# 96 instead of 88 tokens by gathered expert rows, and dense expert products over 160 instead of 168 columns

## The chip, the cores and the metric

The kernel runs on one core of one Trainium2 chip. The metric is the device time of one execution in microseconds, the median of several runs. Everything below is read from one profiled execution, with times in microseconds (us) from the start of its span.

## What is computed

The reference is three transformer layers over 256 tokens of width 1024, in float32. The first has two kinds of attention, the second a state-space mixer, both with a squared-ReLU feed-forward layer. The third has a short convolution and window attention, and then the layer this change is about: a product of experts (PEER) with 16384 experts, of which each token takes 16 in each of 8 heads, 128 in all.

```python
def peer_ffn(h, wq, keys, u_tab, v_tab):        # u_tab, v_tab: 16384 x 1024
    ...
        q = (ht @ wq).reshape(t, PEER_HEADS, 2, PEER_DK)
        sa = jnp.einsum('thd,hnd->thn', q[:, :, 0], keys[0])
        sb = jnp.einsum('thd,hnd->thn', q[:, :, 1], keys[1])
        va, ia = lax.top_k(sa, PEER_TOPK)
        vb, ib = lax.top_k(sb, PEER_TOPK)
        ...
        top, pos = lax.top_k(cand, PEER_TOPK)
        eidx = jnp.take_along_axis(cidx, pos, axis=-1)
        g = jax.nn.softmax(top, axis=-1)
        u = u_tab[eidx]
        v = v_tab[eidx]
        a = jax.nn.gelu(jnp.einsum('thkd,td->thk', u, ht))
        return jnp.einsum('thk,thkd->td', g * a, v)
```

## The kernel before

The kernel is one program with an instruction list written out for each engine; the engines meet by counted semaphores, and each works its list strictly in order. There is no scheduler. The first 750 us are the first two layers and the attention of the third; the change touches none of it. The expert layer divides the 256 tokens in two.

**Dense tokens.** For the first ND tokens (168) all 16384 experts are computed. The table u comes in 128 units of 512 KB (`peer_u`), v in 128 units (`peer_v`). The hidden activations X have a place for 128 x ND numbers on each partition, and what isn't chosen is multiplied by a gate of zero. `u_unit` makes 8 float32 matmuls of 128 x ND for one unit; each shows as two records in the trace. The gates are made by "spreads": for 4 tokens at a time, `one_hot` builds one-hot rows from the chosen numbers (VectorE, GpSimd and ScalarE share this), 4 matmuls of 128 x 128 make the gate matrix of these tokens in PSUM, and VectorE (`empty_gates`, `u_late`) and ScalarE multiply it onto X. There are ND / 4 spreads.

**Gathered tokens.** For the other tokens (88) only the chosen expert rows are read. One "pass" handles 128 chosen rows, so there are as many passes for u as tokens, and again as many for v. GpSimd issues an indirect DMA of 128 rows of 4 KB (`gather`) into one of four slots; VectorE then multiplies the slot with the token's row and sums it (u, `scalar_tensor_tensor` over 1024 elements at L2206) or adds the slot, scaled, to an accumulator (v, L1429). A gather may be issued when the pass four before it is done:

```python
if n >= 4:
    e.wait_ge(*rows_v["pass", n - 4])
```

The passes are in four groups by `ROW_FIRST = (0, 32, 64, 80, 80 + LAST_ROWS)`: in the last one, LAST_ROWS tokens (8) have their 128 choices divided into LAST_PARTS (16) parts over the partitions.

**The order of the work** comes from the constants `N_FIRST` (16), `N_BETWEEN` (23), `N_LATE` (100) and `N_EARLY` (42), by hand-written loops:

- Choice of experts: VectorE finds the top 16 (`pick`), with passes 0 to 15 between; TensorE meanwhile does the first 42 units of u.
- Gate stage: passes 16 to 22, then `spread_steps`. That is a list of 4 x 43 = 172 half units of u, over which the spreads and the passes 23 to N_LATE - 1 are laid:

```python
if (row - N_BETWEEN) * (n_left - 12) < (i - 3) * (N_LATE - N_BETWEEN) and row < N_LATE:
    yield "row", row
```

  The dense products of two units take a PSUM bank (two banks take turns); the bank is free when ScalarE's gelu has been made, and that waits for VectorE where the X of the same place is to be gated.
- Down stage (`down_T`): 256 chunks of v, each half a unit. ScalarE rounds a chunk to its high part (`w_hi`), VectorE makes the low part (`w_lo`, L1423), and TensorE makes for each of 4 blocks a product of w_hi with high and low part of X (2 x ND columns) and one of w_lo with the high part (ND columns). Four chunks can be cut ahead. In VectorE's list the passes from N_LATE on stand between the chunks:

```python
def pass_step(n):
    return 1 + 250 * (n - N_LATE) // (N_PASS - N_LATE)
```

SyncE loads the units in order, each when its raw buffer is free: four buffers for u, eight for v.

Of the kernel before, what the change touches and what calls it, by code (L numbers as in the profile page):

```python
# [21 lines left out]
NHL = 4  # L22
AHEAD = 3
N_EARLY = 42
ND = 168
LAST_ROWS = 8
LAST_PARTS = 128 // LAST_ROWS

OFF_X = 0
# [110 lines left out]
def build(nc, T, out):  # L140
    with ExitStack() as ctx:
        build_in(ctx, nc, T, out)


def build_in(ctx, nc, T, out):
# [82 lines left out]
    def sm(name, p1=128):  # L228
        o, n = SML[name]
        return ar[0:p1, OFF_SM + o:OFF_SM + o + n]  # L230
# [48 lines left out]
    first_v = next(i for i, x in enumerate(plan) if x[0] == "peer_v")  # L279
    DEEP = (128 * ND, OFF_GB + 1024, OFF_HN, OFF_HN + 1024)  # L280

# [249 lines left out]

    X = V(0, 128, ND)
    hT5 = V(20480, 8, 256)
    QP, SCO = 28672, 24576
    hU = V(SCO, 8, ND)

    row_h = [V(SCO + 2048, 1024), V(SCO + 3072, 1024), V(22528, 1024), V(23552, 1024)]
    row_acc, row_out = row_h, V(0, 8, 256)

    ROW_FIRST = (0, 32, 64, 80, 80 + LAST_ROWS)  # L540
    ROW_SUMS = {(24, 0): (0, LAST_ROWS + 16), (48, 0): (1, LAST_ROWS + 48), (60, 0): (2, LAST_ROWS)}
    N_ROWS = ROW_FIRST[4]
    row_g, row_a = [stat(f"rows {n}", N_ROWS) for n in ("gates", "products")]
    row_at = V(OFF_SM + SML["lre"][0], 96)[:, 0:N_ROWS]
    part_rows, part_own, part_sum = sm("cmask"), sm("bones")[:, 0:8], sm("bones")[:, 8:24]
    last_own, last_sum = sm("bones")[:, 24:24 + LAST_PARTS], sm("bones")[:, 24 + LAST_PARTS:24 + LAST_PARTS + LAST_ROWS]
    part_h, last_h, last_rows = V(12288, 8, 128), V(8192, 8, 128), V(9728, 128)

    passes = [("u", p) for p in range(N_ROWS)] + [("v", p) for p in range(N_ROWS)]
    nth = {x: n for n, x in enumerate(passes)}  # L550
    N_PASS, N_FIRST, N_BETWEEN, N_LATE, N_ONES = len(passes), 16, 23, 100, 3
    U_COPY = N_EARLY + 4

    def row_group(p):
# [47 lines left out]
    def spread_steps():  # L602

        n_left, s, emptied, known, late, due, queue = 4 * (64 - N_EARLY // 2), 0, 0, N_EARLY // 2, None, [], []
        n_spread = ND // 4
        i, row = 0, N_BETWEEN
# [33 lines left out]
        assert row == N_LATE and emptied == n_spread  # L640
        yield "late", late, ND

    def sync_program(e):
        e.dma_start(V(OFF_SM, SM_FIRST), T["small"][:, 0:SM_FIRST]).then_inc(small_in, 16)
        e.wait_ge(x_in[0], 16)
        for i, (_, source, _, _) in enumerate(plan):
# [3 lines left out]
            if i == first_v:  # L650
                for s in range(ND // 4 - len(ONES_AT), ND // 4):
                    e.wait_ge(*mm_done["spread", s])
# [766 lines left out]
    def vector_program(e):  # L1419
# [735 lines left out]
        def row_indices():  # L2155
# [8 lines left out]
            own, three = V(OFF_HN + 512, 3, 8, 16), V(OFF_HN + 896, 3, 16)  # L2164
            own2, three2 = V(9216, 3, LAST_PARTS, LAST_ROWS), V(9600, 3, LAST_ROWS)
            e.wait_ge(*mm_done["parts"])
# [1300 lines left out]
```

## Time and profile before

| | |
|---|---|
| median of 3 runs | 1417.73 us (1416.06 to 1417.78) |
| the profiled execution's own time | 1416.42 us |
| its span, first to last instruction | 1414.4 us |
| mean granted TensorE clock | 0.997 of full speed |
| busy: TensorE matmul, VectorE, ScalarE, GpSimd | 1378.1, 1138.3, 775.9, 465.1 us |
| transfers | 371.78 MB, mean 263 GB/s |
| software queue (the gathers) | 97.02 MB |

An engine's busy time is the union of its instructions' records. A matmul's record is longer than the distance to the next one, so the distance of starts tells the pace. What ended an idle time is written in brackets behind a row as the releaser.

### The profile page before, as it was taken

Reading aid. Unit: us, or ns where it says so; the run is one execution under the profiler, and the core shown is the slowest. Engines: PE = TensorE matmul, PEld = TensorE weight load, DVE = VectorE, ACT = ScalarE, POOL = GpSimd, SP = SyncE. Lnnn points to the kernel's source line nnn. Section 1 sums busy time; section 2 is a strip of 40 time slices with the busy share of each in tenths; the row PEclk is TensorE's granted clock in tenths of the full one; section 3 lists DMA queues with packets and bytes.
Section 4 is the critical chain, followed back from the end, with each engine's and each line's share of the span. In section 5 each row is a group of like instructions: output and inputs, shape, how many; then the busy total and the mean of one; then the engine's idle time right before and its main releaser. Section 6 shows DMA issues by size and latency. Waiting matters only on the chain.

```text
span 1414.4 us, 28160 instructions
## 1 busy us (share of the span) xinstructions
PE 1378.1 (97%) x10837; PEld 1283.3 (91%) x10837; DVE 1138.3 (80%) x2315; ACT 775.9 (55%) x1576; POOL 465.1 (33%) x436
## 2 busy tenths in 40 slices
PE   9899999998999999999999999899999999999998
PEld 7678998877889998888889999899999999999998
DVE  5776996787768889877667999576777699999997
ACT  6875886853255455577464301234333366666665
POOL 7700001000200000001100033688878358567671
PEclk9999999999999999999999999999999999999999
DMA  8305554652369899853444599999999999999994
GB/s 269 97 16 183 175 173 146 193 183 64 126 209 348 311 332 333 311 160 108 123 134 137 166 353 368 364 353 384 381 376 369 376 391 402 399 369 394 398 379 158
DMA packets 102579, 371.78 MB, mean 263 GB/s; under 512 B 11424, under 2 KB 11568, under 8 KB 102320
## 3 DMA queue, kind: packets, MB, share of 16 engines
q1 hardware_dynamic: 68096, 245.71, 49.2%
q0 software_dynamic: 26576, 97.02, 18.0%
q10 hardware_dynamic: 7776, 27.27, 5.4%
q8 instruction: 88, 1.44, 0.4%
q14 instruction: 43, 0.35, 0.1%
HBM read 368.90 MB, written 1.05 MB: 262 GB/s over the span
## 4 chain that ended last, share of the span: by engine, by line
PE 80%; DVE 12%; ACT 3%; DMA 2%; issue 2%; POOL 1%; DVEq 0%; SPq 0%; ACTq 0%
PE ps L668 78%; DVE arena L1423 4%; DVE w_lo L1423 2%; DVE arena L2206 1%; DMA arena<-in_u_rows,arena 1%; ACT arena L2350 1%; ACT w_hi L2353 1%; PE ps L886 1%; DVE arena L2109 1%; DVE arena L2033 1%; DVE arena L2031 1%; DVE arena L2030 1%; DMA arena<-in_peer_v 1%; ACT arena L2353 1%; PE ps L1013 0%
## 5 line engine op out<-in xcount | busy, mean ns | idle before, releaser
L2353 ACT ACTIVATE w_hi<-arena 128x512 fp32r<-128x512 f32 x680 | 422.4, 627 | 270.4 <-PE ps L668 254.5
L1423 DVE TENSOR_TENSOR w_lo<-arena,w_hi 128x512 fp32r<-128x512 f32 x680 | 454.7, 691 | 136.2 <-ACT w_hi L2353 132.9
L668 PE MATMUL ps<-act_hi_lo,w_hi 128*128 128x256 f32 (+1 forms) x2496 | 546.3, 313 | 4.8 <-DVE w_lo L1423 2.2
L668 PE MATMUL ps<-arena 128*128 128x168 f32 (+7 forms) x4798 | 469.9, 279 | 17.2 <-ACT arena L2350 7.4
L668 PEld LDWEIGHTS ps<-arena 128*128 128x128 f32 (+3 forms) x4798 | 442.8, 166 | 39.3 <-issue 21.1
L668 PE MATMUL ps<-act_hi_lo,w_lo 128*128 128x168 f32 (+1 forms) x1760 | 455.1, 259 | 0.1
L668 PEld LDWEIGHTS ps<-act_hi_lo,w_hi 128*128 128x128 f32 x2496 | 421.1, 190 | 10.1 <-issue 4.2
L668 PEld LDWEIGHTS ps<-act_hi_lo,w_lo 128*128 128x128 f32 x1760 | 336.7, 191 | 0.2 <-issue 0.2
L668 PE MATMUL ps<-w_hi,act_hi_lo 128*128 128x512 f32 (+2 forms) x960 | 300.7, 389 | 7.5 <-DVE w_lo L1423 3.2
L3270 POOL DMA_INDIRECT arena<-in_v_rows,arena x88 | 190.4, 2163 | 111.5 <-DVE arena L1429 105.5
L668 PEld LDWEIGHTS ps<-w_hi,act_hi_lo 128*128 128x128 f32 x960 | 179.3, 188 | 49.0 <-issue 9.7
L1423 DVE TENSOR_TENSOR arena<-arena 128x512 f32<-128x512 f32 (+16 forms) x306 | 182.0, 603 | 43.8 <-ACT arena L2350 36.8
L668 PE MATMUL ps<-w_lo,act_hi_lo 128*128 128x512 f32 (+2 forms) x480 | 184.7, 385 | 0.0
L3270 POOL DMA_INDIRECT arena<-in_u_rows,arena x88 | 104.3, 1185 | 172.9 <-DVE arena L2029 92.8
L2353 ACT ACTIVATE arena<-ps 128x512 f32<-128x512 f32 (+20 forms) x160 | 70.9, 459 | 135.7 <-DVE arena L1423 102.4
L2350 ACT ACTIVATE arena<-arena 128x128 f32<-128x128 f32 (+9 forms) x247 | 119.4, 498 | 43.8 <-DVE arena L1423 21.3
L2206 DVE SCALAR_TENSOR_TENSOR arena<-arena 128x1024 f32<-128x1024 f32 x88 | 108.8, 1240 | 36.5 <-DMA arena<-in_u_rows,arena 33.5
L2350 ACT ACTIVATE arena<-ps 128x512 f32<-128x512 f32 (+24 forms) x141 | 54.6, 417 | 150.4 <-PE ps L668 126.0
L1429 DVE SCALAR_TENSOR_TENSOR arena<-arena 128x1024 f32<-128x1024 f32 (+5 forms) x110 | 117.0, 1064 | 3.7 <-DMA arena<-in_v_rows,arena 2.9
L668 PEld LDWEIGHTS ps<-w_lo,act_hi_lo 128*128 128x128 f32 x480 | 90.3, 188 | 16.6
L3281 POOL TENSOR_SCALAR arena<-arena 128x128 f32<-128x128 f32 x63 | 83.4, 1328 | 3.1 <-DVE arena L2124 1.5
L3099 POOL TENSOR_TENSOR act_hi_lo<-arena,act_hi_lo 128x256 fp32r<-128x256 f32 x4 | 4.1, 1022 | 242.6 <-ACT act_hi_lo L2353 242.6
(106 smaller groups left out, 723.6 us busy)
## 6 DMA issues: line engine op xcount, KB each, us to landing
arena<-in_w_ff SPq DMA_DIRECT2D x128, 512.0 KB
arena<-in_peer_u SPq DMA_DIRECT2D x128, 512.0 KB
arena<-in_peer_v SPq DMA_DIRECT2D x128, 512.0 KB
arena<-in_w_ada ACTq DMA_DIRECT2D x48, 512.0 KB, 6.5
arena<-in_w_glu SPq DMA_DIRECT2D x16, 512.0 KB
arena<-in_peer_wq SPq DMA_DIRECT2D x16, 512.0 KB
arena<-in_w_in SPq DMA_DIRECT2D x12, 512.0 KB
arena<-in_w_conv SPq DMA_DIRECT2D x12, 512.0 KB
```

Source lines behind the costliest of these rows:

```text
L668: return e.matmul(o, l, r, start=start, stop=stop)
L886: ins = e.transpose(pb(bk, 2 * nk, 128)[:, h * nk + kb, :], att.s(u)[:, h, kb * 128:(kb + 1) * 128], ident)
L1423: return e.tensor_tensor(o, a, b, op)
L1429: return e.scalar_tensor_tensor(out=o, in0=a, scalar=s, in1=b, op0=op0, op1=op1)
L2030: lambda src, tv, ti, tmp: e.max_index(ti[:, 0:8].bitcast(U32), tv[:, 0:8], src),
L2031: lambda src, tv, ti, tmp: e.match_replace(tmp, tv[:, 0:8], src, NEG * 10),
L2033: lambda src, tv, ti, tmp: e.max_index(ti[:, 8:16].bitcast(U32), tv[:, 8:16], tmp)]
L2206: ins = e.scalar_tensor_tensor(out=slot, in0=slot, scalar=1.0, in1=row_h[g], op0=ALU.mult, op1=ALU.mult, accum_out=a)
L2350: return e.activation(o, a, f, **k)
L2353: return e.activation(o, a, ACT.Copy)
L3270: e.indirect_dma_start(row_slot(n), None, T[f"{kind}_rows"], bass.IndirectOffsetOnAxis(ap=row_at[:, p:p + 1].bitcast(U32), axis=0)).then_i ...
L3281: ins = e.tensor_scalar(ob[:, k, :], iota, ibT[:, n:n + 1], gT[:, n:n + 1], ALU.is_equal, ALU.mult)
```

## The change

Eight tokens go from the dense part to the gathered one: ND is 160, LAST_ROWS 16, LAST_PARTS therefore 8. There are 96 passes for u and 96 for v (88 before), 40 spreads (42 before), and N_LATE is 108, so that 85 passes lie in the spread steps (77 before) and 84 in the down stage (76 before). X is 8 columns narrower.

```diff
@@ -22,8 +22,8 @@
 NHL = 4
 AHEAD = 3
 N_EARLY = 42
-ND = 168
-LAST_ROWS = 8
+ND = 160
+LAST_ROWS = 16
 LAST_PARTS = 128 // LAST_ROWS
@@ -548,7 +548,7 @@
     passes = [("u", p) for p in range(N_ROWS)] + [("v", p) for p in range(N_ROWS)]
     nth = {x: n for n, x in enumerate(passes)}
-    N_PASS, N_FIRST, N_BETWEEN, N_LATE, N_ONES = len(passes), 16, 23, 100, 3
+    N_PASS, N_FIRST, N_BETWEEN, N_LATE, N_ONES = len(passes), 16, 23, 108, 3
     U_COPY = N_EARLY + 4
```

VectorE's list at the start of the spread steps, before and after in one piece. L2206 is a pass of u; a TENSOR_TENSOR of 128x512 with the TENSOR_SCALAR behind it is a one-hot; one that reads ps is the gating of a spread, and the 128x2x4 and 128x2x8 are `u_late`, which ScalarE's next gelu waits for.

```order
 L1423 TENSOR_TENSOR arena<-ps,arena 128x48x4
+L2206 SCALAR_TENSOR_TENSOR arena<-arena 128x1024
 L1423 TENSOR_TENSOR arena<-arena 128x2x4
-L2206 SCALAR_TENSOR_TENSOR arena<-arena 128x1024 x2
+L2206 SCALAR_TENSOR_TENSOR arena<-arena 128x1024
 L1423 TENSOR_TENSOR arena<-arena 128x512
 L1426 TENSOR_SCALAR arena<-arena 128x128
 L1423 TENSOR_TENSOR arena<-ps,arena 128x50x4
+L2206 SCALAR_TENSOR_TENSOR arena<-arena 128x1024
 L1423 TENSOR_TENSOR arena<-arena 128x2x8
-L2206 SCALAR_TENSOR_TENSOR arena<-arena 128x1024
```

A pass now stands ahead of `u_late` at these places, and there are more passes for each one-hot.

GpSimd's list at the same place: the gathers (L3270) and the one-hots (L3281). First before, then after.

```order
L3270 DMA arena<-in_u_rows,arena 128x1024 x7
L3281 TENSOR_SCALAR arena<-arena 128x128 x2
L3270 DMA arena<-in_u_rows,arena 128x1024 x2
L3281 TENSOR_SCALAR arena<-arena 128x128
L3270 DMA arena<-in_u_rows,arena 128x1024
L3281 TENSOR_SCALAR arena<-arena 128x128 x2
```

```order
L3270 DMA arena<-in_u_rows,arena 128x1024 x7
L3281 TENSOR_SCALAR arena<-arena 128x128 x2
L3270 DMA arena<-in_u_rows,arena 128x1024 x2
L3281 TENSOR_SCALAR arena<-arena 128x128
L3270 DMA arena<-in_u_rows,arena 128x1024 x3
L3281 TENSOR_SCALAR arena<-arena 128x128 x2
```

Here three gathers stand between two one-hots where there was one; up to this place the lists are the same.

VectorE's list in the middle of the down stage, first before, then after. L1429 is a pass of v, w_lo the low part of a chunk.

```order
L1429 SCALAR_TENSOR_TENSOR arena<-arena 128x1024
L1423 TENSOR_TENSOR w_lo<-arena,w_hi 128x512 x3
L1423 TENSOR_TENSOR act_hi_lo<-arena,act_hi_lo 128x2x168
L1423 TENSOR_TENSOR w_lo<-arena,w_hi 128x512
L1429 SCALAR_TENSOR_TENSOR arena<-arena 128x1024
L1423 TENSOR_TENSOR w_lo<-arena,w_hi 128x512 x3
L1423 TENSOR_TENSOR act_hi_lo<-arena,act_hi_lo 128x2x168
```

```order
L1429 SCALAR_TENSOR_TENSOR arena<-arena 128x1024
L1423 TENSOR_TENSOR w_lo<-arena,w_hi 128x512 x3
L1423 TENSOR_TENSOR act_hi_lo<-arena,act_hi_lo 128x2x160
L1429 SCALAR_TENSOR_TENSOR arena<-arena 128x1024
L1423 TENSOR_TENSOR w_lo<-arena,w_hi 128x512 x3
L1429 SCALAR_TENSOR_TENSOR arena<-arena 128x1024
```

Before, a pass came every three or four chunks; after, nearly always every three.

## Rows read from the trace of the kernel before

**Rows 1.** The page, the span in 40 equal slices.

```profile
PE   9899999998999999999999999899999999999998
...
DVE  5776996787768889877667999576777699999997
...
GB/s 269 97 16 183 175 173 146 193 183 64 126 209 348 311 332 333 311 160 108 123 134 137 166 353 368 364 353 384 381 376 369 376 391 402 399 369 394 398 379 158
```

**Rows 2.** Windows: busy us (instructions) of each engine, granted clock, DMA share, GB/s.

```profile
core 0: us, PE busy (x) PEld busy (x) DVE busy (x) ACT busy (x) POOL busy (x), PEclk, DMA share, GB/s
877.00:1126.00 249.00, 242.91 (x1755) 241.45 (x1755) 172.17 (x328) 87.51 (x260) 186.10 (x147) 0.99 0.98 370
940.00:1100.00 160.00, 160.00 (x1179) 160.00 (x1178) 119.44 (x231) 60.82 (x184) 132.05 (x106) 1.00 1.00 378
900.00:910.00 10.00, 9.54 (x70) 9.24 (x68) 4.73 (x7) 0.00 (x0) 3.46 (x4) 1.00 1.03 409
1127.00:1403.00 276.00, 275.73 (x2072) 275.43 (x2073) 270.76 (x397) 183.49 (x317) 170.78 (x72) 1.00 0.96 373
```

**Rows 3.** Groups by form, TensorE, 940 to 1100 us: busy, mean ns, idle before.

```profile
L668 PE MATMUL ps<-arena 128*128 128x168 f32 x931 | 138.0, 306 | 0.0
L668 PE MATMUL ps<-arena 128*128 128x128 f32 x248 | 32.7, 275 | 0.0
```

**Rows 4.** Timeline of TensorE: start, duration, and idle time before it.

```profile
877.19 0.55 PE L1203 MATMUL ps<-arena 128*128 128x128 f32 x3 [1.35 <-DVE arena L1423]
...
914.97 20.30 PE L668 MATMUL ps<-arena 128*128 128x168 f32 x134 [5.43 <-ACT arena L2350]
...
1200.41 0.35 PE L668 MATMUL ps<-act_hi_lo,w_hi 128*128 128x336 f32 x1
...
1200.60 0.24 PE L668 MATMUL ps<-act_hi_lo,w_lo 128*128 128x168 f32 x1
...
1200.68 0.35 PE L668 MATMUL ps<-act_hi_lo,w_hi 128*128 128x336 f32 x1
```

**Rows 5.** Timeline of VectorE: passes 22, 28, 36, 55 and 99.

```profile
895.63 1.22 DVE L2206 SCALAR_TENSOR_TENSOR arena<-arena 128x1024 f32<-128x1024 f32 x1 [0.95 <-DMA arena<-in_u_rows,arena]
...
911.53 1.23 DVE L2206 SCALAR_TENSOR_TENSOR arena<-arena 128x1024 f32<-128x1024 f32 x1 [1.32 <-DMA arena<-in_u_rows,arena]
...
935.37 1.23 DVE L2206 SCALAR_TENSOR_TENSOR arena<-arena 128x1024 f32<-128x1024 f32 x1 [1.07 <-DMA arena<-in_u_rows,arena]
...
986.49 1.22 DVE L2206 SCALAR_TENSOR_TENSOR arena<-arena 128x1024 f32<-128x1024 f32 x1
...
1111.28 1.27 DVE L1429 SCALAR_TENSOR_TENSOR arena<-arena 128x1024 f32<-128x1024 f32 x1
```

**Rows 6.** GpSimd: one gather's row, and groups by form, 940 to 1100 us.

```profile
902.25 0.94 POOL L3270 DMA_INDIRECT arena<-in_u_rows,arena  x1 [1.61 <-DVE arena L2206]
...
L3281 POOL TENSOR_SCALAR arena<-arena 128x128 f32<-128x128 f32 x48 | 62.4, 1306 | 1.2
L3270 POOL DMA_INDIRECT arena<-in_u_rows,arena x47 | 59.5, 1266 | 20.2 <-DVE arena L2206 12.6 <-issue 7.6
L3270 POOL DMA_INDIRECT arena<-in_v_rows,arena x11 | 13.0, 1186 | 6.6 <-DVE arena L1429 4.6 <-issue 1.3 <-DVE arena L2206 0.5
```

**Rows 7.** Groups by form, VectorE, 940 to 1100 us: the passes of u.

```profile
L2206 DVE SCALAR_TENSOR_TENSOR arena<-arena 128x1024 f32<-128x1024 f32 x50 | 62.3, 1248 | 15.1 <-DMA arena<-in_u_rows,arena 12.2 <-issue 2.6
```

**Rows 8.** Timeline of TensorE: the last dense u products, ending at 1125.84.

```profile
1109.70 16.14 PE L668 MATMUL ps<-arena 128*128 128x168 f32 x112
```

**Rows 9.** Down stage, VectorE: groups of 1140 to 1380, two rows of its timeline.

```profile
L1423 DVE TENSOR_TENSOR w_lo<-arena,w_hi 128x512 fp32r<-128x512 f32 x221 | 142.9, 689 | 3.0 <-ACT w_hi L2353 2.5 <-issue 0.3
...
L1423 DVE TENSOR_TENSOR act_hi_lo<-arena,act_hi_lo 128x336 fp32r<-128x336 f32 x55 | 27.8, 506 | 0.0
...
1385.90 1.28 DVE L1429 SCALAR_TENSOR_TENSOR arena<-arena 128x1024 f32<-128x1024 f32 x1
1387.09 1.29 DVE L1423 TENSOR_TENSOR w_lo<-arena,w_hi 128x512 fp32r<-128x512 f32 x2
```

## The prediction

> **What bounds the kernel now.** I read the page's slices first. From slice 23 on (815 us) TensorE, VectorE and the transfers are all near their tops at once [rows 1], so the share of busy time doesn't say who sets the pace, and the stages have to be read apart. All of the change lies in three of them: the choice of experts (778 to 877 us), the gate stage (877 to 1126 us: dense products with peer_u, one-hot "spreads", row passes 16 to 99) and the down stage (1127 to 1403 us: dense products with peer_v, row passes 100 to 175).
>
> The windows of the last two come next [rows 2]. In the gate stage TensorE is busy 243 of 249 us, VectorE 172, GpSimd 186. In the down stage TensorE is busy all the time, and VectorE 270.8 of 276 us. So TensorE sets the pace in both, but in the down stage VectorE has only 5.2 us to spare in 276, and in the gate stage two things stand close behind TensorE: the ring of four gather slots, and GpSimd.
>
> The ring is seen in the passes' own rows [rows 5]. A pass can start when its gather has landed; the gather into the same slot, four passes on, is issued when the pass is done. Pass 22 starts at 895.63 and pass 28 at 911.53: six periods of 2.65 us, and in this stretch every pass waits for its gather (each row ends with a DMA releaser). The loop is closed by the gather issued at 902.25, which releases pass 28 9.3 us later [rows 5, 6]. TensorE stops for 5.4 us before 914.97 [rows 4], because the gating on VectorE stands behind those passes in its queue. Passes 36 to 55 (935.37 to 986.49, 19 periods) still come every 2.69 us, behind their due time. Over the whole stage, passes 22 to 99 take 77 periods of 2.80 us. In 940 to 1100 VectorE stands 12.2 us before passes for gathers [rows 7].
>
> **What the change takes from TensorE.** In the gate stage the dense product has 8 columns fewer. 931 records of 168 columns and 248 of 128 fill 160 us [rows 2, 3]; taken in proportion to columns a record of 168 is 0.143 us, one of 128 0.109 us, and one of 160 0.136 us. The 86 units of this stage have 16 records each: 1376 x 0.0067 = 9.2 us less. Spreads go from 42 to 40, 8 records of 0.109 us each: 1.7 us less. Together 10.9 us. The first 42 units save another 4.5 us, but they run beside the choice of experts, where VectorE is the chain (TensorE waits for it 1.35 us at 877 [rows 4]), so I count them at nothing; if they were on the path, they would be worth 4.5 us at most.
>
> In the down stage one pair of products (336 and 168 columns) starts every 0.27 us at the full clock [rows 2, 4], where 504 columns at 2.4 GHz make 0.21. What the rest is the trace doesn't say. If it stays, 24 columns fewer save 0.010 us a pair, and 1024 pairs 10.2 us; if the second product is bound by its weight load, only 16 columns count, 6.8 us. The Trainium skill (TensorE: Matmul & The Clock Gate, Back-to-back issue gap) gives N/2.4 + 2.5 ns for one product, so by an estimate from that page the pair would take 0.215 us; the trace has 0.27, and the saving by the page's rule is again 0.010 us a pair.
>
> **What it adds.** 8 passes on expert rows of u and 8 of v, each with a gather of 512 KB. N_LATE goes from 100 to 108, so that 85 instead of 77 passes stand in the spread steps and 84 instead of 76 in the down stage.
>
> *Gate stage.* The steps are 172 half units, and the passes are laid over the first 160 of them. A half unit is 8 records of 0.143 and its share of the spreads, 0.21: 1.36 us now, 1.29 then. So passes are due every 2.83 us now and every 2.43 then. The ring must be asked whether it can do 2.43. It has never done so over a stretch: 2.65 at the start, 2.69 in passes 36 to 55. GpSimd has in 940 to 1100 per pass a gather (72.5 us over 58) and its share of the one-hots (62.4 us over 58), 2.33 us, and 0.15 us of issue ahead of each gather (8.9 us over 58) [rows 6]; with fewer one-hots for each pass (40 spreads for 85 passes, 42 for 77) that is 1.25 + 0.93 + 0.15 = 2.33 us, 96% of the due rate. The transfers would have to bring 262 KB of weights in each half unit and 278 KB of rows, 0.54 MB in 1.29 us: 418 GB/s, where the best ten microseconds here have 409 and the stage 370 [rows 2]. Nothing here can do the due rate with ease, so I take the ring's measured 2.65 us. Pass 22 stays where it is (the order up to it is unchanged), so pass 107 comes at 895.6 + 85 x 2.65 = 1120.9. Eleven half units of the program stand behind the last u-stage pass (now 14.6 us from 1111.28 to TensorE's last product at 1125.84 [rows 5, 8]; 11 x 1.36 = 15). TensorE can be up to two PSUM banks ahead of a late VectorE; I take 5 half units of lead, 6 x 1.29 = 7.7 us remain. End 1128.6 against 1125.8: **+2.8 us**. With no lead it is +9, with 8 half units -1. The bounds of the ring: 2.43 (it keeps the due rate: -10.9) and the stage's own mean of 2.80 (+15.5).
>
> *Down stage.* VectorE does 8 passes more. Two start-to-start distances behind a pass are 1.19 us (1385.90 to 1387.09 [rows 9]), so +9.5 us. The low part of the gates (act_hi_lo) has 320 elements instead of 336; 512 take 689 ns and 336 take 506 [rows 9], so 16 elements are 17 ns, over 64 of them -1.1 us. Against 5.2 us to spare that leaves +3.2 us, and as some idle time at the stage's ends can't be used I take **+4 us**. TensorE's 7 to 10 us are then of no use, it waits for w_lo. Bounds: +2, if all of VectorE's idle time fills and its tail is shorter; +8.4, if none fills. Transfers need per chunk of 1.11 us 262 KB and a third of 524 KB, about 395 GB/s, less than the 409 that were carried, and the ring has four periods of 3.3 us there for a gather that took 9.3, so I put nothing there.
>
> *The rest.* The reduction of the last group has 48 outputs instead of 24, three small operations are wider: at most 0.1 us in the chain at 812. Output: the last products have 16 columns instead of 8, the copies out 160 and 96 instead of 168 and 88: nothing.
>
> **Sum**: 2.8 + 4 = +6.8 us. The profiled execution took 1416.42 us, which gives 1423.2; the median of the runs is 1.3 us above it, 1424.5. I forecast 1424.
>
> **Rivals.** (1) *The gathers keep up.* When TensorE and its weights slow down for a moment, the ring gets more of the transfers and heals itself. Then the gate stage gains its 10.9 us, the down stage loses 4: -7, 1411 us. For it: passes 22 to 99 came every 2.80 us on average where 2.83 were due, so the late start was made up. Against it: the 418 GB/s. The Trainium skill (DMA: Bandwidth & Descriptors, Where 436 GB/s comes from) has two figures: about 358 GB/s from HBM, which ten microseconds of 409 contradict, and a fabric ceiling of 435. By the ceiling 418 would fit, and this rival would hold. Chance 0.2. (2) *The ring runs at 2.56 us*, the shortest distance that repeats while gathers are waited for: 895.6 + 217.6 + 7.7 = 1120.9, -4.9, and with the down stage -1: 1417. Chance 0.15. (3) *The ring stretches* to 2.80: more one-hots, gathers and weights collide, +15.5 + 4: 1437. For it: the gather took 9.3 us where the transfers were at 409 GB/s. Chance 0.15. (4) *VectorE is no floor in the down stage*, because its records are longer than what it really needs: then TensorE's 7 to 10 us come through, with +2.8 before them -4 to -7: 1411 to 1413. Against it: the start-to-start distances count, not the durations, and they fill the stage. Chance 0.05. My forecast keeps 0.45.
>
> **How the numbers follow.** The measurement tells 0.2% (2.8 us) from no change. Faster: rivals 1 and 4, 0.24 with a little of 2. Same, 1415 to 1420.5: rival 2 and the low edge of the forecast, 0.2. Slower: most of the forecast and rival 3, 0.56. The forecast's own range is 1418 to 1431. To leave out no more than 2 in 10 the range has to take in rival 1 at 1411 and reach to rival 3: 1410 to 1436.
>
> **What would show it.** The dense record of 160 columns at 0.136 us in its spacing, and a pair of the down stage at 0.257 to 0.26 us where nothing waits. Pass 22 still near 895, passes then every 2.65 us and nearly all of them waiting for a gather, TensorE with stops of several us in the gate stage (5.4 now). The last dense u product at about 1128. In the down stage VectorE at 99% or more and TensorE with small stops for w_lo, 280 us long. The prediction is wrong if passes come every 2.45 us without waits (rival 1), or if the down stage is shorter than 276 us (rival 4).

## The result: slower by 16 us, and the profile after

| | before | after |
|---|---|---|
| median | 1417.76 us (4 runs, 1416.06 to 1421.73) | 1433.89 us (4 runs, 1433.29 to 1440.20) |
| ratio to before | 1 | 1.0121, 95% interval 1.0103 to 1.0138 |
| span of the profiled execution | 1414.4 us | 1431.5 us |
| mean granted TensorE clock | 0.997 | 0.993 |

The change is slower, as forecast, and the time is inside the range. But the loss is 16.1 us where the forecast of 1424 had 6.3. The span grew by 17.1 us.

The page's slices of the changed kernel (40 slices of the span, busy share in tenths; the last line is what the transfers moved):

```profile
PE   9899999998999999999999998899999899999998
...
DVE  5766996788669889867668898567777699999998
...
GB/s 267 96 21 182 176 176 148 192 179 45 152 222 348 312 325 342 261 164 103 120 157 154 182 384 329 361 400 377 368 382 386 368 387 398 400 391 397 402 390 180
```

TensorE, at 9 in nearly all slices before [rows 1], now has gaps in the gate stage, and the transfers run at 387 to 402 GB/s in the slices of the down stage, the last one left out (369 to 402 before). The windows of the same kernel, with the columns of [rows 2]: the gate stage, its middle, its busiest ten microseconds, the down stage.

```profile
877.00:1136.00 259.00, 238.56 (x1739) 235.63 (x1739) 178.33 (x341) 80.56 (x250) 190.74 (x153) 0.97 0.97 370
940.00:1100.00 160.00, 151.42 (x1133) 150.29 (x1132) 115.22 (x230) 51.70 (x168) 128.69 (x102) 0.99 0.99 380
900.00:910.00 10.00, 9.97 (x76) 9.70 (x75) 4.94 (x8) 1.33 (x3) 3.52 (x4) 1.00 1.02 412
1138.30:1414.00 275.70, 273.28 (x2030) 266.08 (x2031) 272.56 (x396) 178.53 (x310) 198.43 (x80) 0.99 1.00 389
```

In the gate stage TensorE stands for 20.4 of 259 us, where it stood for 6.1 of 249. In the down stage the roles have changed: VectorE has 3.1 us of gaps (5.2 before), TensorE 2.4 (0.3 before).

VectorE's timeline of the changed kernel gives the passes. These are pass 22, the next two, pass 28 (911.09), and the last four of the gate stage up to pass 107:

```profile
898.24 1.23 DVE L2206 SCALAR_TENSOR_TENSOR arena<-arena 128x1024 f32<-128x1024 f32 x1 [3.50 <-DMA arena<-in_u_rows,arena]
...
900.67 1.23 DVE L2206 SCALAR_TENSOR_TENSOR arena<-arena 128x1024 f32<-128x1024 f32 x1 [1.20 <-DMA arena<-in_u_rows,arena]
...
903.18 1.23 DVE L2206 SCALAR_TENSOR_TENSOR arena<-arena 128x1024 f32<-128x1024 f32 x1 [1.27 <-DMA arena<-in_u_rows,arena]
...
911.09 1.23 DVE L2206 SCALAR_TENSOR_TENSOR arena<-arena 128x1024 f32<-128x1024 f32 x1 [1.31 <-DMA arena<-in_u_rows,arena]
...
1118.10 2.67 DVE L1429 SCALAR_TENSOR_TENSOR arena<-arena 128x1024 f32<-128x1024 f32 x2
...
1123.23 1.28 DVE L1429 SCALAR_TENSOR_TENSOR arena<-arena 128x1024 f32<-128x1024 f32 x1
...
1125.00 1.28 DVE L1429 SCALAR_TENSOR_TENSOR arena<-arena 128x1024 f32<-128x1024 f32 x1
```

From pass 22 to pass 107 are 85 periods in 226.8 us, 2.67 each. The group of the same passes in 940 to 1100 shows who made them late (12.2 us of waiting for gathers before [rows 7]):

```profile
L2206 DVE SCALAR_TENSOR_TENSOR arena<-arena 128x1024 f32<-128x1024 f32 x58 | 72.1, 1250 | 32.0 <-DMA arena<-in_u_rows,arena 31.8
```

The chain that ended last, between 870 and 1136 us of the changed kernel, shows the loop of the ring: a gather is issued by GpSimd (L3270), lands some 8 to 9 us later, a pass runs, and the next gather is issued, with one-hots (L3281) between (columns: start, duration, what). TensorE is in it at the very end only, for 3.3 us.

```profile
889.87 1.63 POOL arena L3270
891.80 8.85 DMA arena<-in_u_rows,arena
900.67 1.25 DVE arena L2206 x2
902.18 8.89 DMA arena<-in_u_rows,arena
911.09 1.25 DVE arena L2206 x2
913.58 2.88 POOL arena L3281 x2
916.62 1.83 POOL arena L3270
```

TensorE's timeline at both ends of the gate stage (changed kernel): the first stop for the gating, as long as before (5.24 against 5.43 us [rows 4]), the last stops, and the start of the down stage. The stop before 1123.32 ends when GpSimd's one-hots are done (1121.63 to 1123.22), which stand in its list behind a gather's issue.

```profile
899.79 12.43 PE L668 MATMUL ps<-arena 128*128 128x160 f32 x92
917.45 17.84 PE L668 MATMUL ps<-arena 128*128 128x160 f32 x111 [5.24 <-ACT arena L2350]
...
1117.83 3.31 PE L668 MATMUL ps<-arena 128*128 128x160 f32 x24 [0.57 <-ACT arena L2350]
1123.32 12.38 PE L668 MATMUL ps<-arena 128*128 128x128 f32 x88 [2.18 <-issue]
1138.25 0.44 PE L668 MATMUL ps<-act_hi_lo,w_hi 128*128 128x320 f32 x1 [2.55 <-DVE act_hi_lo L1423]
1138.48 0.34 PE L668 MATMUL ps<-act_hi_lo,w_lo 128*128 128x160 f32 x1
1138.62 0.55 PE L668 MATMUL ps<-act_hi_lo,w_hi 128*128 128x320 f32 x1
...
1139.10 0.55 PE L668 MATMUL ps<-act_hi_lo,w_hi 128*128 128x320 f32 x1
```

The last dense u product ends at 1135.70 (before at 1125.84 [rows 8]). The down stage's first product comes 2.55 us later (before 1.32), and its pairs start 0.48 us apart for the first 3.3 us, with TensorE's granted clock at half after the stops; at 1141.5 they go back to 0.26. VectorE waits there for a high part from ScalarE, which waits for TensorE:

```profile
1141.02 0.69 DVE L1423 TENSOR_TENSOR w_lo<-arena,w_hi 128x512 fp32r<-128x512 f32 x1 [1.02 <-ACT w_hi L2353]
```

What the down stage's first product waits for is the first load of peer_v, then its cutting (2.6 us in both kernels). SyncE issues it in its order behind the last load of peer_u, and that one waits until TensorE has freed a buffer, at 1126.64 in the changed kernel and 1116.22 before. The same piece of the chain in the changed kernel, then in the kernel before:

```profile
1127.11 8.50 DMA arena<-in_peer_v
```

```profile
1116.70 7.80 DMA arena<-in_peer_v
```

TensorE's own last four units take 9.1 us from there, 9.6 before, so it has to stop in both kernels, and its narrower products only make the stop longer.

From its first product to the first transpose of the output the down stage takes 286.8 us, 280.9 before. So the 17.1 us of the span are 9.9 in the gate stage, 1.2 at the change of stages and 6.0 in the down stage.

VectorE's groups in the down stage, 1150 to 1390 us, of the changed kernel. No wait is left but 1.1 us:

```profile
L1423 DVE TENSOR_TENSOR w_lo<-arena,w_hi 128x512 fp32r<-128x512 f32 x217 | 139.9, 684 | 1.1 <-ACT w_hi L2353 1.1
L1429 DVE SCALAR_TENSOR_TENSOR arena<-arena 128x1024 f32<-128x1024 f32 x70 | 89.5, 1278 | 0.0
L1423 DVE TENSOR_TENSOR act_hi_lo<-arena,act_hi_lo 128x320 fp32r<-128x320 f32 x55 | 26.6, 484 | 0.0
```

### The profile page after: what moved, and what is told of

Same layout as the page of the kernel before. It is cut to its first block, busy times and chain, and to the rows that moved or that the text cites. A ratio compares the mean times of both kernels' runs of the same rounds, so it can differ in the third digit from the quotient of the medians.

```text
span 1431.5 us, 28153 instructions
## 1 busy us (share of the span) xinstructions
PE 1375.1 (96%) x10821; PEld 1270.6 (89%) x10821; DVE 1151.5 (80%) x2333; ACT 767.1 (54%) x1568; POOL 496.3 (35%) x449
## 4 chain that ended last, share of the span: by engine, by line
PE 65%; DVE 15%; DMA 9%; POOL 5%; issue 4%; ACT 3%; DVEq 0%; SPq 0%; ACTq 0%
PE ps L668 63%; DMA arena<-in_u_rows,arena 6%; DVE arena L1423 5%; POOL arena L3270 3%; DVE arena L2206 2%; POOL arena L3281 2%; DVE w_lo L1423 2%; ACT arena L2350 1%; DMA arena<-in_v_rows,arena 1%; ACT w_hi L2353 1%; DVE arena L1429 1%; PE ps L886 1%; DVE arena L2109 1%; ACT arena L2353 1%; DMA arena<-in_peer_v 1%
## 5 line engine op out<-in xcount | busy, mean ns | idle before, releaser
L668 PE MATMUL ps<-arena 128*128 128x160 f32 (+8 forms) x4782 | 464.1, 279 | 29.8 <-ACT arena L2350 17.0
L668 PEld LDWEIGHTS ps<-arena 128*128 128x128 f32 (+3 forms) x4782 | 434.3, 168 | 54.7 <-issue 34.2
L668 PE MATMUL ps<-act_hi_lo,w_lo 128*128 128x160 f32 (+1 forms) x1760 | 451.8, 257 | 0.5 <-DVE w_lo L1423 0.5
L3270 POOL DMA_INDIRECT arena<-in_v_rows,arena x96 | 220.7, 2299 | 86.8 <-DVE arena L1429 79.9
L3270 POOL DMA_INDIRECT arena<-in_u_rows,arena x96 | 116.9, 1218 | 184.6 <-DVE arena L2029 92.7
L2353 ACT ACTIVATE arena<-ps 128x512 f32<-128x512 f32 (+19 forms) x158 | 70.2, 460 | 184.0 <-DVE arena L1423 153.0
L2206 DVE SCALAR_TENSOR_TENSOR arena<-arena 128x1024 f32<-128x1024 f32 x96 | 118.5, 1242 | 52.8 <-DMA arena<-in_u_rows,arena 52.6
L1429 DVE SCALAR_TENSOR_TENSOR arena<-arena 128x1024 f32<-128x1024 f32 (+6 forms) x118 | 127.0, 1076 | 3.2 <-DMA arena<-in_v_rows,arena 2.6
L2350 ACT ACTIVATE arena<-ps 128x512 f32<-128x512 f32 (+25 forms) x141 | 53.7, 412 | 122.3 <-PE ps L668 121.8
L3099 POOL TENSOR_TENSOR arena<-arena 128x32 f32<-128x32 f32 (+1 forms) x130 | 55.6, 442 | 81.4 <-ACT arena L2353 46.4
```

What stands on the lines that cost most here:

```text
L668: return e.matmul(o, l, r, start=start, stop=stop)
L1429: return e.scalar_tensor_tensor(out=o, in0=a, scalar=s, in1=b, op0=op0, op1=op1)
L2206: ins = e.scalar_tensor_tensor(out=slot, in0=slot, scalar=1.0, in1=row_h[g], op0=ALU.mult, op1=ALU.mult, accum_out=a)
L2350: return e.activation(o, a, f, **k)
L2353: return e.activation(o, a, ACT.Copy)
L3099: return e.tensor_tensor(o, a, b, op)
```

## The experiments

"u end" is the end of the last dense u product; "down stage" is from its first product to the first transpose of the output; a period is from pass 22 to the last pass of the gate stage, over their number. "First search" is the start of VectorE's first search for the largest scores (MAX8, L2029 before and after), which stands before anything that the change or an experiment touches. All in us, from the profiled execution; times are medians beside runs of the kernel before on the same chip. Two kernels had one run only, and no interval.

| run | time | ratio (95%) | first search | pass 22 | period | u end | down stage |
|---|---|---|---|---|---|---|---|
| before | 1417.8 to 1419.2 | 1 | 743.4 | 895.6 | 2.80 | 1125.8 | 280.9 |
| after | 1433.9 | 1.0121 (1.0103 to 1.0138) | 744.3 | 898.2 | 2.67 | 1135.7 | 286.8 |
| late100 | 1425.3 | 1.0046 (1.0028 to 1.0064) | 744.1 | 898.5 | 2.76 | 1120.6 | 295.0 |
| wide_columns | 1434.6 | 1.0100 (1.0064 to 1.0136) | 744.0 | 896.7 | 2.72 | 1140.2 | 286.1 |
| half_gathers | 1412.2, one run |  | 744.0 | 896.3 | 2.46 | 1115.9 | 285.6 |
| five_slots | 1421.8 | 1.0026 (1.0009 to 1.0042) | 747.1 | 899.1 | 2.51 | 1123.4 | 286.8 |
| pool_relief | 1426.8 | 1.0059 (1.0038 to 1.0080) | 744.6 | 897.3 | 2.59 | 1127.9 | 285.6 |
| five_relief | 1418.8 | 0.9997 (0.9979 to 1.0015) | 743.8 | 897.9 | 2.50 | 1120.1 | 286.6 |
| half_v_passes | 1422.3, one run |  | 743.3 | 897.6 | 2.67 | 1135.9 | 275.6 |
| five_slots_168 | 1421.4 | 1.0023 (0.9999 to 1.0048) | 745.5 | 898.5 | 2.79 | 1128.3 | 282.0 |
| narrow_only | 1418.0 | 0.9991 (0.9962 to 1.0021) | 746.4 | 898.8 | 2.76 | 1122.3 | 295.6 |
| narrow_gate | 1416.4 | 0.9983 (0.9961 to 1.0005) | 744.3 | 898.4 | 2.74 | 1122.1 | 284.2 |
| narrow_down | 1426.8 | 1.0034 (1.0008 to 1.0061) | 742.6 | 894.6 | 2.77 | 1122.5 | 295.4 |
| narrow_half_v | 1406.3 | 0.9913 (0.9887 to 0.9940) | 744.4 | 898.1 | 2.73 | 1119.3 | 273.8 |

The first search comes between 742.6 and 747.1 us, so pass 22 and the u end of one execution carry some 2 us either way that no edit made; the period and the down stage don't. Its rows, first before, then after:

```profile
743.38 0.48 DVE L2029 MAX8 arena<-arena 128x8 f32<-128x128 f32 x2
```

```profile
744.30 0.48 DVE L2029 MAX8 arena<-arena 128x8 f32<-128x128 f32 x2
```

The theory: after loses in the gate stage because the ring of four slots can't bring 85 passes in the time, and in the down stage because VectorE is full; TensorE's saving is idle in both. The rivals: TensorE or the weights bound the gate stage, the transfers bound the down stage.

### late100: the eight passes moved out of the gate stage

```diff
-    N_PASS, N_FIRST, N_BETWEEN, N_LATE, N_ONES = len(passes), 16, 23, 108, 3
+    N_PASS, N_FIRST, N_BETWEEN, N_LATE, N_ONES = len(passes), 16, 23, 100, 3
```

> The changed kernel with N_LATE back at 100: 77 passes in the spread steps instead of 85, 92 in the down stage instead of 84. Ring theory (gate stage paced by the four gather slots at 2.67 us a pass): passes are then due every 2.69 us, so the ring just keeps up, pass 99 comes near 1104 and the last dense u product near 1119 instead of 1135.7, some 17 us earlier. VectorE theory of the down stage (each pass costs 1.2 us there): 8 passes more make it 9.6 us longer, 297 instead of 287. Together about -7 us against the changed kernel, 1426. If VectorE is no floor in the down stage, that stays 287 us and the time is 1417. If the ring isn't what paces the gate stage (TensorE or the total of transfers does), its end moves by less than 6 us and the time is 1437 or more.

With 77 passes in the spread steps instead of 85, all else as changed, the u end is 15.1 us earlier, 5.2 before that of the kernel before; TensorE is busy 159.59 of 160 us in 940 to 1100. The down stage has 92 passes and takes 8.1 us more than with 84: 1.02 us for each pass, nearly VectorE's own 1.19. So each pass costs 1.9 us in the gate stage and 1.0 in the down stage. Both came near what was expected (1120.6 for 1119, 295.0 for 297, 1425.3 for 1426).

### wide_columns: TensorE's saving taken away

The changed kernel, TensorE multiplying 168 columns (the last 8 belong to gathered tokens; nobody reads what they give).

```diff
-                ins = mm(pb(j % 2, 2, ND)[:, m, :], w[:, k, :], src[:, k, 0:ND], k == 0, k == 7)
+                ins = mm(pb(j % 2, 2, NW)[:, m, :], w[:, k, :], src[:, k, 0:NW], k == 0, k == 7)
...
-                            mm(pb(k, 2, ND), h[:, cols], both_parts[:, m, :, 0:ND], first, False)
+                            mm(pb(k, 2, NW), h[:, cols], both_parts[:, m, :, 0:NW], first, False)
...
```

> The changed kernel (96 passes, 40 spreads, N_LATE 108), but TensorE multiplies 168 columns of which the last 8 are never used. So only the narrower product is undone. Theory (ring in the gate stage, VectorE in the down stage; TensorE's saving falls into waits): the last dense u product stays within 3 us of 1135.7, the down stage within 2 us of 287, total 1433 to 1438. Rival, TensorE still sets the pace of a good part: 9 us more in the gate stage and 7 to 8 in the down stage, 1450.

By the medians narrower products are worth 0.7 us in the changed kernel; by the ratios (1.0100 against 1.0121, the intervals overlap) the kernel with 168 columns is even the faster one. So nothing measurable came of them, where on paper they took 16 to 19 us of work from TensorE in the two stages (9.2, and 6.8 or 10.2). Of the profiled executions that with 168 columns has its u end 4.5 us later, more than the 3 that were expected, a down stage 0.8 us shorter, and a span 2.3 us longer.

### half_gathers, five_slots, pool_relief: what holds the ring

half_gathers brings only half of each row in passes 23 to 107 (and multiplies the passes' u by 0), so it leaves out half of the gathered transfers there. five_slots gives the ring a fifth slot, in memory that is free from unit 46 on. pool_relief takes a one-hot out of each second spread from GpSimd and gives it to ScalarE. The core of each edit, cut from three kernels:

```diff
...
+            if N_BETWEEN <= n < N_LATE:
+                source, cut = source.rearrange("r (h c) -> (r h) c", h=2), 512
...
-        return V(QP + 1024 * (g % 4), 1024)
+        k = ring(g)[0]
+        return V(QP + 1024 * k if k < 4 else 21504, 1024)
...
-        return "pool" if k == 1 or k == 2 and s % 2 else "scalar"
+        return "pool" if k == 1 else "scalar"
```

> The changed kernel, in which gathers 23 to 107 fetch only 512 of 1024 elements of a row (half the bytes, as many packets) and the u passes after 22 multiply by zero: it leaves out the products of these passes, their instructions stay the same. Ring and transfer theories both expect the landings to come in about 5 us and the passes to reach the due 2.43 us: the gate stage ends near 1122 instead of 1135.7, total 1420. If GpSimd sets the period (gather and one-hots in its order), it stays at 2.5 to 2.67 us and the end at 1129 to 1136.

> The changed kernel with a fifth gather slot from gather 28 on (in 1024 words that the narrower X and the dead first input leave free). The bytes are the same. Ring theory (four slots, each taken for a landing of 8 us and 2.6 us until its next gather is issued): the loop with five gives (8.2 + 2.6) / 5 = 2.2 us, under the due 2.43, so the passes keep up, the gate stage ends 10 to 14 us earlier (1122 to 1126), total about 1421. Rival, the sum of transfers is the limit (0.54 MB for each half unit at 409 GB/s): landings only get later (10 us instead of 8), the period stays above 2.55, and no more than 3 us come back, 1431. Rival, GpSimd is the limit: period 2.5, 5 to 7 us come back.

> The changed kernel with a third of GpSimd's one-hots (20 of 60) given to ScalarE. Ring theory with the next gather's issue as part of the loop: the one-hots in GpSimd's list delay issues by 2.6 us on average, with a third fewer by about 2.2; period (8.2 + 2.2) / 4 = 2.60, gate stage 5 us shorter, total 1428. If only the landing counts, nothing: 1433. If GpSimd's own load were the limit (2.33 us a pass) it would fall to 2.0 and the passes reach the due 2.43: 13 us, 1420.

With half the bytes the ring keeps almost the due rate of 2.43 us (2.46), and the u end is 10.0 us before that of the kernel before: this is about what rival 1 promised, 10.9, and 6 us more than was expected of this run, which is a single one. With whole rows and a fifth slot it does 2.51, and the u end is 12.3 us earlier than in the changed kernel. With four slots and fewer one-hots on GpSimd it does 2.59, 7.8 us earlier. The windows 940 to 1100 of half_gathers, five_slots and pool_relief, in this order:

```profile
940.00:1100.00 160.00, 157.32 (x1196) 156.68 (x1196) 122.69 (x238) 56.33 (x183) 137.97 (x110) 1.00 0.89 301
```

```profile
940.00:1100.00 160.00, 158.86 (x1203) 157.59 (x1202) 125.78 (x242) 56.16 (x183) 132.38 (x109) 1.00 1.03 407
```

```profile
940.00:1100.00 160.00, 153.83 (x1161) 152.40 (x1161) 120.63 (x238) 66.36 (x207) 118.74 (x91) 1.00 1.01 390
```

Five slots carry 407 GB/s over 160 us, where four carried 380. So "the transfers are full" was not what the changed kernel's 0.99 of DMA share said: more gathers under way moved 7% more. Three things make the ring's period (slots, landing time, what stands between gathers on GpSimd), and easing any of them shortens it.

### five_relief: both together

> The changed kernel with a fifth gather slot and, beside it, fewer one-hots on GpSimd; a whole version. Each alone took 12.1 and 7.1 us off the changed kernel's 1433.9. If GpSimd is what still holds the ring of five: pass 107 at 1108 to 1109, last dense u product at 1120 to 1121, time 1419. If the transfers do (1.03 of their time busy, 407 GB/s, with five slots): nothing is gained, pass 107 at 1110 to 1111, 1421 to 1422. In neither case does it beat the kernel before by 0.2%, since the down stage keeps its 286 to 287 us.

The edits of five_slots and pool_relief together. The u end comes at 1120.06, as expected of GpSimd holding the ring of five. The last pass stands at 1110.07, which reads like the other branch, but the expectation's pass times were counted one pass early: in five_slots pass 106 is at 1110.78 and pass 107 at 1112.55. The time is that of the kernel before, 0.9997 (0.9979 to 1.0015): the gate stage is 5.8 us shorter than before, the down stage 5.7 us longer. This is the best whole version with 96 gathered tokens that I found, and it beats nothing.

### half_v_passes: what holds the down stage

It leaves out half of what the v passes of the down stage add; the gathers stay whole.

```diff
-                ins = stt(row_acc[g], slot, a, row_acc[g], ALU.mult, ALU.add)
+                cut = 512 if n >= N_LATE else 1024
+                ins = stt(row_acc[g][:, 0:cut], slot[:, 0:cut], a, row_acc[g][:, 0:cut], ALU.mult, ALU.add)
```

> The changed kernel, in which the v passes of the down stage add only the first 512 of 1024 elements (it leaves out half of these sums; gathers and everything else stay). VectorE theory: 80 passes cost 0.6 us instead of 1.2, 48 us less, so that TensorE sets the pace of the down stage: 256 chunks of 4 x 0.26 us and the small row sums, 268 instead of 287 us, total about 1414. Rival, the transfers set its pace (396 GB/s): nothing changes, 1433.

The down stage is 11.2 us shorter, with the same transfers; so VectorE holds it, not the transfers. (GpSimd's issues become shorter too, 1.20 us on average for 2.51, but in the changed kernel VectorE never waited for a gather in this stage.) But it gives less than expected, because the transfers stand right behind. Its window 1150 to 1390, and ScalarE's group of the high parts, which now waits 22.9 us for peer_v:

```profile
1150.00:1390.00 240.00, 239.53 (x1838) 238.49 (x1838) 218.20 (x361) 160.52 (x282) 91.21 (x76) 1.00 1.03 409
```

```profile
L2354 ACT ACTIVATE w_hi<-arena 128x512 fp32r<-128x512 f32 x226 | 140.6, 631 | 79.8 <-PE ps L668 51.5 <-DMA arena<-in_peer_v 22.9 <-issue 1.0
```

### five_slots_168, narrow_only: two misses on the kernel before

five_slots_168 is the kernel before with the fifth slot for passes 24 to 98, and peer_v's first load waits for pass 98. narrow_only is the kernel before, all dense products over 160 columns (it leaves out the last 8 dense tokens).

```diff
-                ins = mm(pb(j % 2, 2, ND)[:, m, :], w[:, k, :], src[:, k, 0:ND], k == 0, k == 7)
+                ins = mm(pb(j % 2, 2, ND)[:, m, 0:160], w[:, k, :], src[:, k, 0:160], k == 0, k == 7)
...
-                            mm(pb(k, 2, ND), h[:, cols], both_parts[:, m, :, 0:ND], first, False)
+                            mm(pb(k, 2, ND)[:, :, 0:160], h[:, cols], both_parts[:, m, :, 0:160], first, False)
...
```

> The kernel before with a fifth gather slot for the passes 24 to 98 of the gate stage; 168 columns and 88 passes as before. Ring theory: the passes are due every 2.83 us and the loop can do 2.2, so VectorE is not late any more after its start; what it can give is part of TensorE's stop of 5.4 us near 910. 1 to 4 us, total 1414 to 1417. Rival: the stop comes from passes 20 to 28, which still have four slots, nothing changes, 1417.

> The kernel before (88 passes, 42 spreads, N_LATE 100) with products over 160 columns: it leaves out the last 8 dense tokens in TensorE's products alone, all else stays. What the narrower product is worth by itself. Due period of the passes 1.29 x 160 / 77 = 2.68 us, just what the ring does (2.67): the gate stage ends 7 to 9 us before 1125.8; down stage 281 - 5 = 276, where VectorE's work of 271 stands; total 1404 to 1407. Rival, it is worth all of TensorE's saving, 9 + 7 us: 1401 or less. Rival, nothing, because transfers bind already: 1416.

Neither gained. With 77 passes the period, 2.79, is near the 2.83 of the due times, so a fifth slot has little to shorten; 1 to 4 us were expected, and 1.0023 (0.9999 to 1.0048) is rather the other way. Its u end is 2.4 us later than before, but its first search was 2.1 us later already. narrow_only should have gained 10 us and gave nothing: its runs lie between 1412.4 and 1431.7, and in its profile (an execution of 1428.0 us) the down stage takes 295.6 us though TensorE's work is less. Its GpSimd has two gather issues of 13.64 and 14.33 us there, where the kernel before has none over 3.6. That led to the last three.

### narrow_gate, narrow_down, narrow_half_v: where the narrower product goes

The edit of narrow_only in the gate stage alone, in the down stage alone, and in both together with the halved v passes of half_v_passes.

> The kernel before (88 gathered tokens), with the dense products of the gate stage alone over 160 columns; the down stage's stay at 168. It leaves out the products of the last 8 dense tokens in the hidden layer. Theory (what narrower products in the gate stage are worth is real but small, since passes then wait for the ring, and the down stage must not be touched): the last dense u product 3 to 6 us before 1125.8, the down stage 281 us long as before, no gather issue over 4 us, time 1412 to 1415, runs close together. Rival (the spread and the nil result of the narrower kernel came from the gate stage): 1416 to 1420, with runs spread over 10 us.

> The kernel before, with the dense products of the down stage alone over 160 columns (it leaves out the last 8 dense tokens in the output's product). Theory (TensorE then no longer holds VectorE back, VectorE runs without a gap for long stretches, and GpSimd's gather issue, 2.4 us on average, waits through such a stretch; VectorE then runs dry, TensorE stops and its clock falls to half): at least one gather issue of over 8 us in the down stage, ended by VectorE's own wait for the gathered rows, the stage 278 to 296 us long, runs spread over more than 10 us, median 1414 to 1422. Rival (the long issues in the narrower kernel were chance, and TensorE's saving of 7 to 10 us comes through up to VectorE's 5 us): no issue over 4 us, stage 275 to 277 us, time 1412 to 1413, runs within 4 us.

> The kernel before, with all dense products over 160 columns as in the narrower kernel, and the row passes of v in the down stage on 512 of 1024 elements (it leaves out the other half of what they add, and the last 8 dense tokens). Theory (a VectorE without gaps is what held up the gather issues): issues in the down stage 1.0 to 1.3 us on average and none over 4, the stage 270 to 273 us long (TensorE's saving comes through, 281 less 7 to 10), time 1404 to 1410, runs close together. Rival (the long issues come from something else, as the transfers): some issues over 8 us again, the stage over 280 us, time 1412 to 1420.

narrow_gate: the u end is 3.7 us earlier, the time 0.9983 of before, whose interval takes in 1. Here the expectation was too good: one gather issue of 9.99 us stood in the down stage too, which is 284.2 us long, and the runs spread over 8 us. narrow_down: less work for TensorE, and 4.8 us slower by the ratio (1.0008 to 1.0061), 7.6 by the medians; its ten runs lie between 1413.0 and 1431.8, and the down stage of the profiled one is 295.4 us. Its windows through the first event, with the granted clock in the third last place:

```profile
1160.00:1168.00 8.00, 7.89 (x61) 7.73 (x60) 8.00 (x13) 5.38 (x10) 6.68 (x3) 1.00 1.00 396
1168.00:1176.00 8.00, 8.00 (x63) 7.91 (x62) 8.00 (x12) 5.60 (x10) 8.00 (x1) 1.00 0.91 304
1176.00:1184.00 8.00, 4.36 (x34) 4.17 (x33) 2.31 (x5) 3.53 (x6) 5.93 (x4) 0.94 0.78 254
1184.00:1192.00 8.00, 4.57 (x19) 4.60 (x20) 5.91 (x8) 1.06 (x2) 2.76 (x2) 0.50 0.90 331
```

and its timelines of GpSimd, VectorE and TensorE there:

```profile
1161.88 3.37 POOL L3270 DMA_INDIRECT arena<-in_v_rows,arena  x1 [0.66 <-DVE arena L1429]
1165.91 13.21 POOL L3270 DMA_INDIRECT arena<-in_v_rows,arena  x1 [0.66 <-DVE arena L1429]
...
1164.34 1.29 DVE L1429 SCALAR_TENSOR_TENSOR arena<-arena 128x1024 f32<-128x1024 f32 x1
...
1174.79 1.29 DVE L1429 SCALAR_TENSOR_TENSOR arena<-arena 128x1024 f32<-128x1024 f32 x1
...
1177.01 1.31 DVE L1423 TENSOR_TENSOR w_lo<-arena,w_hi 128x512 fp32r<-128x512 f32 x2
1185.40 1.28 DVE L1429 SCALAR_TENSOR_TENSOR arena<-arena 128x1024 f32<-128x1024 f32 x1 [7.09 <-DMA arena<-in_v_rows,arena]
...
1187.43 0.61 PE L668 MATMUL ps<-act_hi_lo,w_hi 128*128 128x320 f32 x1 [7.08 <-DVE w_lo L1423]
```

A gather's issue begins at 1165.91 and ends at 1179.12, 0.8 us after VectorE has run out of work (1177.01 and 1.31). The two long issues of narrow_only and the other one of narrow_down end in the same way, and that of narrow_gate without a dry VectorE. Until then VectorE has no gap. The issue before it, 3.37 us long, shows what is usual: it ends at 1165.25, 0.9 us after the start of a row pass of VectorE. In 1150 to 1390 us all 64 of the changed kernel's issues of over 2.2 us end 0.9 us after the start of a pass, and 44 of 49 in the kernel before; so an issue runs on beside the w_lo and act_hi_lo products and ends in the next pass. Four w_lo products between two passes give 3.37 us, three give 2.35 or 2.75. The long issue ran past the passes at 1167.76, 1170.77 and 1174.79 instead. No further gather can be issued, the transfers fall to 254 GB/s, VectorE stands 7.09 us for its rows, TensorE 7.08 us for w_lo, and its clock goes to half. narrow_half_v gives VectorE gaps: 65 issues of 1.14 us on average in 1150 to 1390 (64 of 2.63 us in narrow_down) and none over 1.5. The down stage takes 273.8 us, 7.1 less than before, and the kernel 0.9913. I read this as TensorE's saving coming through; halved passes beside 168 columns were not run, but TensorE had only 0.3 us of gaps to give there [rows 2]. What was expected, 270 to 273 us, was a little too good.

```profile
L3271 POOL DMA_INDIRECT arena<-in_v_rows,arena x65 | 74.3, 1142 | 151.5 <-DVE arena L1429 140.1 <-DVE arena L1426 7.9 <-issue 3.4
```

The Trainium skill (SBUF — State Buffer, SBUF: two separate sides) says that VectorE and GpSimd share a pair of ports. A VectorE instruction in a 2-port mode holds the pair for its whole length, and so does one with two inputs from SBUF against a GpSimd instruction that reads SBUF. A DMA issued by GpSimd is held up by a 2-port one, because its descriptors can't be written. The w_lo products and the passes have two inputs from SBUF; which of the two cases this is, no run shows. The trace agrees in kind: issues are long beside a full VectorE. The page has the one that waits free again when VectorE's instruction ends; here a 3.37 us issue outlasted several and a 13 us issue some twenty of them, so the measurement decides.

## Why the prediction was right or wrong

**Right: the direction and both bounds.** The ring's 2.65 us were taken from six periods at the start of the stage, and the stage had 2.67 over 85. In the down stage VectorE took TensorE's place as the bound: half_v_passes and late100 show it from both sides. TensorE's saving is of no use there (wide_columns). "The gathers keep up" (rival 1) fell by the ring and not by its other premise: half_gathers shows that the gain of 10 us is there for a ring that keeps the due rate. The 418 GB/s that this asks for were not carried over 940 to 1100 us in any run: five_relief comes nearest, 408 GB/s and 2.50 us.

**Wrong: the sizes.** The sum had +6.8 and the span got +17.1. By the prediction's steps:

1. *"Pass 22 stays where it is (the order up to it is unchanged)"*: it came at 898.24, +2.6. Little of this need be the change's: 0.9 us stood already at the first search, before anything that the change touches. From there pass 22 comes after 152.3 us before and 153.9 after, and the twelve other kernels have 151.9 to 154.4, those of 168 columns and of 160 mixed. I should have given this term bounds.
2. *"passes at 2.65"*: 2.67, which makes +1.5 over 85 periods.
3. *"I take 5 half units of lead, 7.7 us remain"*: 10.7 us remained behind pass 107, +3.0. This is the step that failed: of eleven half units at 1.29 us TensorE had less than three ahead. Five half units were chosen without a row, and no run has them: in the nine other kernels with 160 columns in the gate stage 9.8 to 12.4 us remain, 10.8 of them in half_gathers, whose ring keeps nearly the due rate. So it isn't the late ring that takes the lead away, and what does is open.
4. The change of stages was costed at nothing and took 1.2 us. The down stage begins when the first load of peer_v has landed and been cut: this load took 8.50 us instead of 7.80, and TensorE's last four units 0.6 us less, so its stop grew by both. The prediction had no such path.
5. *Down stage "+4"*: +6.0, inside the bounds of +2 to +8.4. VectorE kept 3.1 us of its gaps instead of the 0.8 that my sum left it. 1.4 of them are two waits for w_hi behind TensorE's half clock (1141.02 and 1143.89; in the same place 0.25 before). The prediction saw TensorE's stops and did not price what the clock loses after them.

The first three make the gate stage +9.9 instead of +2.8, and this is most of the miss, though the first of them need not be the change's. Rival 3 (+15.5 + 4, 1437) had the total nearer, but by a period of 2.80 us that did not come.

**What stays open.** Why a few gather issues run past two to four passes of VectorE and take 10 to 14 us, where most end in the next pass after 2.35 to 3.37. It isn't the narrower product alone: five_slots_168, with 168 columns, has one of 5.77 us that ran past one pass. The changed kernel has VectorE just as full and none over 3. So the long issues explain the narrower kernels' loss, not the changed kernel's.

## What to carry to other kernels

Where an engine's work is cut and another engine stands 2% behind it, look for who becomes the bound before counting the saving: here 16 to 19 us of TensorE's work were worth nothing that the runs could tell from noise. When a ring of buffers falls behind its due rate, everything behind it is late to the end. Take the lead of an engine from rows and not from what its buffers allow, follow the chain through the change of stages (here a load of 8 us), and add what the clock loses after a stop. A full DMA share with a ring that waits does not mean that the transfers are at their top: ask what one more slot would do, since it moved 7% more here.

## What the runs showed of the hardware

- GpSimd's issue of an indirect DMA of 128 rows took 1.14 us while VectorE had gaps, mostly 2.35, 2.75 or 3.37 us where it had next to none, and five times, in narrow_only, narrow_gate and narrow_down, 9.99 to 14.33 us. Four of these five ended 0.8 us after VectorE had run dry. The issues of over 2.2 us otherwise ended, nearly all, 0.9 us after the start of VectorE's next row pass over 1024 elements (64 of 64 in the changed kernel, 1150 to 1390), and ran on through the tensor_tensor products before it.
- TensorE's clock was at half for 3.3 us after a stop of 2.55 us that followed others (1138.25 in the changed kernel), and for 6 us after one of 7.08 us in narrow_down.
- One core's transfers ran at 407 and 408 GB/s over 160 us with five slots.
- Less work on TensorE alone made the kernel slower (narrow_down, 1.0034; 1.0008 to 1.0061), by two issues of 13.2 us in the profiled execution. That VectorE's short gaps had kept the issues short before is argued, not shown: the changed kernel has fewer gaps and no long issue.
